# Expert rows gathered as 4 slots of 32 tokens, and summed by a 128x32 matrix on a quarter of the array's columns

## What is computed

```
sc, ci = lax.top_k(cand, PEER_TOPK)                    # 16 of 256 candidates, per token and head
e = i1[ci // 16] * N_KEYS + i2[ci % 16]                # expert number
g = jax.nn.softmax(sc, axis=-1)
# per block of 128 tokens, hk = 8 * 16 = 128 experts per token
a = jax.nn.gelu(jnp.einsum('tkd,td->tk', u[eb], xb))   # one dot product per token and expert
y = jnp.einsum('tk,tkd->td', a * gb, v[eb])            # weighted sum of the experts' v rows
```

## Time and profile before

| | us |
|---|---|
| median of 3 runs (5132.05 to 5136.66) | 5132.38 |
| the profiled execution's own time | 5135.75 |
| its span, first to last instruction | 5133.9 |
| busy in the span: PE / DVE / ACT / POOL | 3980.3 / 2828.7 / 1475.3 / 1408.6 |
| gathers of layer 0, first issue to the end of the loop | about 935 to 2615 |
| gathers of layer 1 | about 3457 to 5098 |

### The profile page before, as it was taken

How to read it: one execution, slowest core, us unless ns; L and a number is a source line. 1 busy time by engine, 2 the same in 40 slices (tenths; PEclk the granted TensorE clock), 3 DMA queues, 4 the chain that set the end, 5 groups by cost and what they waited for, 6 DMA issues and landing times.

```text
span 5133.9 us, 41619 instructions
## 1 busy us (share of the span) xinstructions
PE 3980.3 (78%) x13660; PEld 1858.4 (36%) x13660; DVE 2828.7 (55%) x6023; ACT 1475.3 (29%) x4303; POOL 1408.6 (27%) x1477
## 2 busy tenths in 40 slices
PE   8789979887777777777767897867777777777776
PEld 1365636222222222223234655442322222322222
DVE  2443364665675765755455333556657667576544
ACT  1224433222222222232222344222222222222222
POOL 1011100233343343433320111003333434334332
PEclk9887889999999999999988868889999999999999
DMA  8110011999999999999951000119999999999997
GB/s 260 64 39 1 1 42 66 366 414 414 418 408 410 417 410 408 413 416 392 419 184 50 15 1 9 62 39 404 403 412 414 410 420 403 408 415 419 415 420 294
DMA packets 214073, 1460.14 MB, mean 284 GB/s; under 512 B 23968, under 2 KB 24224, under 8 KB 49248
## 3 DMA queue, kind: packets, MB, share of 16 engines
q0 software_dynamic: 186496, 1355.11, 64.6%
q1 hardware_dynamic: 27360, 102.37, 5.9%
HBM read 1453.19 MB, written 4.19 MB: 284 GB/s over the span
## 4 chain that ended last, share of the span: by engine, by line
PE 42%; DMA 37%; DVE 12%; ACT 5%; issue 4%; SPq 0%; POOL 0%; DVEq 0%; ACTq 0%; POOLq 0%
DMA work<-expert_dram,work 27%; PE psum L649 17%; PE psum L448 10%; DMA hT<-expert_dram,work 8%; PE psum L554 4%; DVE work L1239 4%; PE psum L538 3%; PE psum L460 2%; ACT work L859 2%; PE psum L515 2%; PE psum L568 2%; DVE hT L1239 1%; DVE work L979 1%; ACT work L849 1%; PE psum L485 1%
## 5 line engine op out<-in xcount | busy, mean ns | idle before, releaser
L649 PE MATMUL psum<-work 128*128 128x512 f32 x3416 | 1613.7, 617 | 534.4 <-ACT work L859 534.4
L1239 DVE SCALAR_TENSOR_TENSOR work<-work,psum 128x1024 f32<-128x1024 f32 x854 | 1041.9, 1220 | 870.0 <-DMA work<-expert_dram,work 857.7
L1297 POOL DMA_INDIRECT work<-expert_dram,work x854 | 830.6, 973 | 1514.8 <-PE psum L649 1341.9
L649 PEld LDWEIGHTS psum<-work 128*128 128x128 f32 x3416 | 628.7, 193 | 1505.8 <-ACT work L859 865.3
L649 PE MATMUL psum<-hT,work 128*128 128x512 f32 x1704 | 810.6, 620 | 316.8 <-ACT work L859 316.7
L849 ACT ACTIVATE work<-work,xinv 128x2 f32<-128x2 f32 x640 | 189.1, 295 | 2385.6 <-DVE work L1239 1575.1
L1239 DVE SCALAR_TENSOR_TENSOR hT<-hT,psum 128x1024 f32<-128x1024 f32 x426 | 519.7, 1221 | 441.8 <-DMA hT<-expert_dram,work 441.6
L1297 POOL DMA_INDIRECT hT<-expert_dram,work x426 | 420.7, 988 | 845.1 <-PE psum L649 673.5
L649 PEld LDWEIGHTS psum<-hT,work 128*128 128x128 f32 x1704 | 315.2, 194 | 804.4 <-ACT work L859 483.1
L448 PE MATMUL psum<-hT,split 128*128 128x128 f16 (+1 forms) x2880 | 435.4, 312 | 58.0 <-DVE hT L1014 58.0
L859 ACT ACTIVATE work<-const,work 128x128 f32<-128x128 f32 x1280 | 434.1, 386 | 0.0
(11 more groups left out here) (152 smaller groups left out, 2868.5 us busy)
## 6 DMA issues: line engine op xcount, KB each, us to landing
ring<-w_mod_dram SPq DMA_DIRECT2D x96, 512.0 KB, 4.8
ring<-w_in_dram SPq DMA_DIRECT2D x40, 512.0 KB, 3.5
ring<-w_query_dram SPq DMA_DIRECT2D x32, 512.0 KB, 3.4
work<-expert_dram,work POOLq DMA_INDIRECT x854, 8.5
ring<-w_out_dram SPq DMA_DIRECT2D x16, 512.0 KB, 3.5
hT<-expert_dram,work POOLq DMA_INDIRECT x426, 8.5
work<-rpb_dram POOLq DMA_DIRECT2D x4, 1344.0 KB, 18.8
xT<-xT_dram SPq DMA_DIRECT2D x1, 2560.0 KB, 11.5
```

Of the source, the lines that this page charges most:

```text
L649: last = pe.matmul(out[:, cols_], diag[:, n % NDIAG, :], rows[n % NBUF][:, D + 512 * half:D + 512 * half + 512], start=(s == 0), stop=(s = ...
L1239: dve.scalar_tensor_tensor(u, u, 1.0, pair[t % 2], ALU.mult, ALU.mult, accum_out=act_in[:, s:s + 1]).then_inc(dot_done, 1)
L1297: pool.indirect_dma_start(rows[n % NBUF], None, a[f"expert{l}"], bass.IndirectOffsetOnAxis(expert[:, t % 2, s:s + 1], 0)).then_inc(row_in[ ...
```

## The change

A transfer now holds 4 slots of 32 tokens. Within a tile the 128 tokens form NG = 4 groups of GR = 32. A transfer brings, for one group, four of its slots: partition 32j+i holds the row of token i of the group for slot j of four. The transfers with even number serve one group, those with odd number another; the first 64 transfers of a tile (HALF) serve groups 0 and 1, the last 64 groups 2 and 3. The number and size of the transfers stay.

- `regroup` (new) moves expert numbers and weights to this layout, with 16 DVE copies of 32x32 for each of the two.
- The dots need each group's tokens four times over the partitions. `turn_tile` transposes the tile to PSUM, ACT copies it to SBUF (`tile_copy`, into `h_tile`), and `spread_rows` multiplies it with a selection matrix `pick`: 4 matmuls of 128x512 for the two groups of a half, into `pair[0]` and `pair[1]`. Those two PSUM pairs are read by all dots of the half, so a spread waits for the last dot of the half before it (`dot_done`).
- The sum over slots of a group uses a 128x32 matrix (`stack` scaled by the numbers), whose output is 32 PSUM partitions, on 32 of the array's 128 columns. The four matmuls of two transfers alternate between the two groups. PE waits for both matrices at once.
- The finished sum is transposed into its own PSUM pair, and the modulation chunks of layer 1 use one PSUM bank in place of two.

```diff
+GR = 32
+NG = P // GR
+HALF = SLOTS // 2
+TURN = HALF - 4
+TILE_SLOT = 116
...
+        def mod_bank(l, c):
+            return 2 + c % 2 if l == 0 else 6
...
-                if q == 0 and NCHUNK * l + c >= 2:
-                    pe.wait_ge(mod_row, NCHUNK * l + c - 1)
+                if q == 0 and NCHUNK * l + c >= (2, 1)[l]:
+                    pe.wait_ge(mod_row, NCHUNK * l + c - (1, 0)[l])
...
+            def spread_rows(l, t, half):
+
+                if half == 0:
+                    pe.wait_ge(tile_in, TT * l + t + 1)
+                    pe.wait_ge(pick_in, l + 1)
+                if t + half > 0:
+                    pe.wait_ge(dot_done, SLOTS * (TT * l + t) + HALF * half)
+                for x in range(2):
+                    for n in range(2):
+                        last = pe.matmul(pair[x][:, 512 * n:512 * n + 512], pick[:, 2 * half + x, :],
+                                         h_tile[:, 512 * n:512 * n + 512], start=True, stop=True)
                 last.then_inc(h_turned, 1)
...
-                    for s in range(SLOTS):
+                    for s in range(0, SLOTS, 2):
...
-                        if s == SLOTS // 2 and t + 1 < TT:
-                            turn_rows(l, t + 1)
-                        pe.wait_ge(diag_done, n + 1)
+                        if s == TURN:
+                            spread_rows(l, t, 1)
+                        if s == TILE_SLOT and t + 1 < TT:
+                            turn_tile(l, t + 1)
+                        if s == HALF + TURN and t + 1 < TT:
+                            spread_rows(l, t + 1, 0)
+                        pe.wait_ge(diag_done, n + 2)
                         for half in range(2):
-                            cols_ = slice(512 * half, 512 * half + 512)
-                            last = pe.matmul(out[:, cols_], diag[:, n % NDIAG, :],
-                                             rows[n % NBUF][:, D + 512 * half:D + 512 * half + 512],
-                                             start=(s == 0), stop=(s == SLOTS - 1))
-                        last.then_inc(row_used, 1)
+                            for x in range(2):
+                                g = 2 * (s // HALF) + x
+                                last = pe.matmul(out[GR * g:GR * g + GR, 512 * half:512 * half + 512],
+                                                 diag[:, (n + x) % NDIAG, :],
+                                                 rows[(n + x) % NBUF][:, D + 512 * half:D + 512 * half + 512],
+                                                 start=(s % HALF == 0), stop=(s % HALF == HALF - 2))
+                                if half == 1:
+                                    last.then_inc(row_used, 1)
...
+            def regroup(dst, src):
+
+                d = dst.rearrange("p (a q x) -> p a q x", a=2, x=2)
+                s = src.rearrange("p (q j) -> p q j", j=NG)
+                for g in range(NG):
+                    for j in range(NG):
+                        last = dve.tensor_copy(d[GR * j:GR * j + GR, g // 2, :, g % 2], s[GR * g:GR * g + GR, :, j])
+                return last
...
-                        if s == 0:
-                            dve.wait_ge(h_turned, TT * l + t + 1)
+                        if s % HALF == 0:
+                            dve.wait_ge(h_turned, 2 * (TT * l + t) + s // HALF + 1)
                         dve.wait_ge(row_in[i % NBUF], 16 * (i // NBUF + 1))
                         u = rows[i % NBUF][:, 0:D]
-                        dve.scalar_tensor_tensor(u, u, 1.0, pair[t % 2], ALU.mult, ALU.mult,
+                        dve.scalar_tensor_tensor(u, u, 1.0, pair[s % 2], ALU.mult, ALU.mult,
```

More of the change, by code:

```diff
@@ L606, in queries, with turn_tile @@
                         last.then_inc(keyscore, 1)
-            def turn_rows(l, t):
+            def turn_tile(l, t):
                 if t >= 2:
                     pe.wait_ge(y_added, TT * l + t - 1)
+                if t == 1 and l + 1 < L:
+                    pe.wait_ge(mod_read, 2 + l + 1)
                 for c in range(KC):
-                    last = pe.transpose(pair[t % 2][:, c * P:(c + 1) * P], y32[:, c, t * P:(t + 1) * P], con("ident"))
+                    last = pe.transpose(pair[2 + t % 2][:, c * P:(c + 1) * P], y32[:, c, t * P:(t + 1) * P], con("ident"))
+                last.then_inc(tile_turned, 1)
+            def spread_rows(l, t, half):
[8 more added lines that the diff above has]
+                                         h_tile[:, 512 * n:512 * n + 512], start=True, stop=True)
                 last.then_inc(h_turned, 1)
@@ L820, in softmax_exp, with tile_copy @@
                 act.activation(sel, sel, ACT.Exp).then_inc(gexp_ready, 1)
+            def tile_copy(l, t):
+                act.wait_ge(tile_turned, TT * l + t + 1)
+                if t > 0:
+                    act.wait_ge(h_turned, 2 * (TT * l + t))
+                act.activation(h_tile, pair[2 + t % 2], ACT.Copy).then_inc(tile_in, 1)
             def sum_copy(l, t):
@@ L829, in experts @@
             def experts(l):
+                act.activation(pick.rearrange("p g (j i) -> p g j i", j=NG),
+                               con("ident").rearrange("p (g i) -> p g i", g=NG).unsqueeze(2).to_broadcast(
+                                   [P, NG, NG, GR]), ACT.Copy).then_inc(pick_in, 1)
+                tile_copy(l, 0)
                 if l + 1 < L:
@@ L847, in experts @@
                             softmax_exp(l, t + 1)
+                        if s == TILE_SLOT + 2 and t + 1 < TT:
+                            tile_copy(l, t + 1)
                         act.wait_ge(dot_done, n + 2)
@@ L1215, in choose @@
                 link(last)
-                dve.scalar_tensor_tensor(expert[:, t % 2, :], route[:, 0, :], float(NK), route[:, 1, :], ALU.mult,
-                                         ALU.add).then_inc(expert_ready, 1)
+                link(dve.scalar_tensor_tensor(route[:, 0, :], route[:, 0, :], float(NK), route[:, 1, :], ALU.mult,
+                                              ALU.add))
+                regroup(expert[:, t % 2, :], route[:, 0, :]).then_inc(expert_ready, 1)
                 if t > 0:
@@ L1248, in residual @@
                         x = xT[:, c, t * P:(t + 1) * P]
-                        last = dve.scalar_tensor_tensor(x, pair[t % 2][:, c * P:(c + 1) * P],
+                        last = dve.scalar_tensor_tensor(x, pair[2 + t % 2][:, c * P:(c + 1) * P],
                                                         modT[:, l, 5 * KC + c, side:side + 1], x, ALU.mult, ALU.add)
@@ L1357, in constants @@
     c["iota"] = np.tile(np.arange(P), (P, 1))
+    c["stack"] = (p[:, None] % 32 == np.arange(32)[None, :])
     c["iota16"] = np.tile(np.arange(16), (P, 1))
```

34 lines of the change are left out of this document (22 added, 12 removed).

## The result

The change makes the kernel slower: 5526.92 us median of 4 runs, against 5134.52 of the kernel before measured beside it, ratio 1.0768 (95% interval 1.0749 to 1.0786). That is **392 us more**, where the prediction said 141 and its range ended at 5335. The direction was right, the size was not.

A forecast was written before the change was run, and what follows sets the result against it. Transfers were taken to bound the loop, one each 2.5 us. Spreads 135, regroup 4.4 and layer 0's start 2 made +141 us on the profiled 5135.75, 5277; against the median it said 5275, range 5205 to 5335.

The forecast's parts named there:

- The bound: Gather loop: transfers bind it, one each 2.5 us, with the six-buffer loop fitting them; halving PE's work buys nothing by itself.
- The spread: Tile middles and boundaries inside a layer: sums wait behind the spread, next gather 9.4 us late; 18 x 7.5 = 135 us.
- cover: Steady gather loop: a gather can be issued 7.7 - 5.8 = 1.9 us later before the DMA engines run dry.
- Regroup and the starts: Layer starts: regroup delays the first gather 2.2 us, twice, 4.4 us; layer 0's dots 4.5 us later, 2 counted lost.
- the steady loop: Sums on 32 columns between spreads: even buffer released 0.3 us later, within the 1.9 us allowed; 0 for all 640 pairs.
- the named rival: PE's clock falls and stays low in the loop: up to 64 us plus 164 us of spreads, 5300 to 5370; chance 0.10.
- No overlap: PE's sums: the two groups' matmuls do not run side by side; 8.5 us a spread, 5290 to 5320; chance 0.27.
- Covered: At the spreads: faster landings hide most of the delay, 18 x 2 to 4 us lost, 5175 to 5215; chance 0.07.
- faster: Gather loop: earlier release of odd buffers holds 422 GB/s throughout, 78 us less, time 5060; chance 0.04.
- none: Whole kernel: no change, gain from earlier release and loss at the spreads equal; chance 0.03.
- Both at once, low clock and no overlap: Steady loop: bound to PE with 7 us a pair, some 1300 us more; chance 0.01.
- two signs of being wrong: Gather behind a spread landing within 2 to 3 us of its usual time, or transfers faster than 422 GB/s.

The follow-up runs named there:

- e4: The change with two unused filler matmuls behind each pair of sums, in slots 24 to 111 of 8 of the 10 tiles: 5370.34 us, ratio 1.0452.
- e3: The change with the spread two transfers later, behind the sums of transfers 60 and 61 (TURN = HALF - 2): 5397.84 us, ratio 1.0512.
- e5: The change with groups served one after another, 32 transfers each, the next group spread early into the idle PSUM pair: 5149.12 us, ratio 1.0029.
- e8: The kernel before, 128-wide sums, with one wait for both matrices of a pair and the matmul order unchanged: 5190.33 us, ratio 1.0121.
- e6: The kernel before, 128-wide sums, with one wait for both matrices of a pair and the two transfers' halves alternating: 5454.05 us, ratio 1.0627.
- e2: The change with a pair's four matmuls in the order of before, both halves of one transfer, then of the next: 5499.57 us, ratio 1.0698.

## Why the prediction was wrong

**The bound: right.** The loop is bound by transfers and by the loop of six buffers, and halving PE's work buys nothing: e4's stretch with overlapped sums at full clock has 0.059 us of excess against 0.062.

**The spread: right in place and mechanism, in size by two errors that cancel.** 7.5 us each and 135 in all were said; 7.3 and 131 measured. At the place shown the four matmuls took 6.45 us (5.4 taken, bound 7.0) and the sums 1.91. Over all 18, the gather behind the spread is 9.8 us late (9.4 said), and it lands 2.6 us faster than before, where 1.9 of cover was taken. That is 7.2 lost. The short landing was the right measure here, since the queue is empty here. e3 confirms the mechanism by taking most of the loss away.

**Regroup and the starts: small, as said.** DVE's timeline of the change at the start of layer 1 has the sixteen copies of the expert numbers:

```profile
3652.28 3.07 DVE L1228 CAST work<-work 32x32 uint32<-32x32 f32 x16
```

3.07 us where 2.2 was taken (bound 3.5). In layer 0 the first gather is hardly later (935.2 for 935.0), and the dots start 6.7 us later where 4.5 was said:

```profile
955.00 1.22 DVE L1303 SCALAR_TENSOR_TENSOR work<-work,psum 128x1024 f32<-128x1024 f32 x1 [14.73 <-PE psum L643]
```

e5, which has the regroup and the spreads, is 15 us above the kernel before.

**The step that failed: "so the steady loop gains nothing; 0.3 lies within the 1.9. I take 0 for all 640 pairs."** It measured 261 us. Two things were wrong in it, the clock at which a pair runs and the cover.

- It priced the pair at the higher clock. The prediction did name the other case (chance 0.10), with a pair of 3.7 us at 1.2 GHz, and that is what happens: 0.71 in the loop. It gave it a low chance without a reason, and against itself: its own list of signs has "PE's clock is then low for much of the loop" if the groups overlap, which was its likeliest case. So its sum and its list of signs did not fit each other.
- It took 1.9 us of cover, from one landing of 5.8 us, so even the named rival came out at only 64 us. The shortest landing was that of a gather with almost nothing else in flight. In the change 18 gathers were issued into an empty queue and landed after 5.2 to 5.7 us, while those with two others in flight took 6.8 (a twentieth took less) to 7.9 (median); in the kernel before, 6.6 to 7.4. Against the 7.7 that I used, the cover is 0.3 to 1.1 us. And the odd gather, on which the chain runs, is issued 1.24 us behind the even one when both come free at once, which the working mentioned and then did not add. e8's 0.3 us cost 1.2%, e6's 1.2 and 0.7 us cost 6.3%. The Trainium skill, DMA: Bandwidth & Descriptors, section Anatomy of one DMA — SWDGE (gpsimd) path, by which I estimated 4.4 us, gives its sum for one DMA; the empty queue shows 5.2 to 5.7 us, and the measurement decides.

The range fell with that step: 5275 + 261 is 5536, 9 us from the measured 5527.

**The rivals and the signs.** No overlap: refuted, 1.91 us for a pair. Covered, faster, none: refuted. "Both at once, low clock and no overlap" did not occur. The clock's fall came, at some four times the 64 us that it was given. The signs at the spreads came: at the 18 places POOL waits 9.7 to 15.2 us for PE, the spreads take 5.2 to 6.8 us, and the gather behind one lands 9.1 us behind the gather before it on average, where that was 2.6. The signs that failed are those of the loop between them: the dots were to follow each 2.5 us and GB/s to fall to 395, and it is 365. Neither of the two signs of being wrong looked at the steady loop, and neither showed.

## What to carry to other kernels

An engine that isn't the bound can still be made too idle: before its work is halved, ask what TensorE's clock does then, and price the work at 1.2 GHz too. When the chain runs through a ring of buffers at the transfers' full rate, the price of a late release is not read from the shortest landing but from landings with the usual number in flight, and it can be near the whole delay (e8). By the same token handing on each buffer as soon as it can be is worth more (1% here) than faster arithmetic. An instruction that waits for later work belongs behind everything that is already due: moving it by one pair gave back 129 us.

## What the hardware showed that I had not expected

- Two transfers' matmuls on different column groups run side by side also when all four records of one stand ahead of those of the other (e2: 1.92 us for eight records), and not on the same group (e5: 3.62).
- PE kept its clock at 1.00 while it worked 3.62 us and rested 1.26 of each pair (e5), and was at the lower level for most of the time when it worked 1.91 and rested some 3 (0.71 over the change's loop). It went to and fro: behind the spread and the sums after it, unbroken work from 1515.13 to 1525.2, the sums ran at the higher level, and the pair at 1535.61, behind a rest of 8.38 us, took 3.63. It also came back without such a stretch: the pair at 1545.42 took 1.91 behind two of 3.63 with rests of 1.33 and 1.24.
- A DMA share of 0.94 to 0.98 went with 365 to 374 GB/s, and 1.01 with 421. The share alone hid a loss of 11 to 13%.
